# mLSTM keys and values brought to the rows of their chunk by a block-wise load and a VectorE transpose, in place of TensorE transposes

## What is computed

```python
s = jnp.einsum('bjhd,bshd->bhjs', q, k) * w
num = jnp.einsum('bhjs,bshe->bjhe', s, v) + inter_blh[..., None] * jnp.einsum('bjhd,bhde->bjhe', q, C)
den = jnp.sum(s, axis=-1).transpose(0, 2, 1) + inter_blh * jnp.einsum('bjhd,bhd->bjh', q, n)
h = num / jnp.maximum(jnp.abs(den), floor)[..., None]
C_new = decay[..., None, None] * C + jnp.einsum('bhs,bshd,bshe->bhde', w_last, k, v)
n_new = decay[..., None] * n + jnp.einsum('bhs,bshd->bhd', w_last, k)
```

## Time and profile before

| | us |
|---|---|
| median of three executions | 1893.55 |
| the profiled execution's own time | 1891.67 |
| its span (first to last instruction) | 1889.9 |
| TensorE busy | 1871.4 (99%) |
| VectorE busy | 1331.9 (70%) |
| ScalarE busy | 873.5 (46%) |
| the mLSTM's steps, first to last transpose | 572.3 to 817.8 |

### The profile page before, as it was taken

One profiled execution on the slowest core, in us unless ns is written; L12 is line 12 of the kernel. 1 busy time (PEld: TensorE's weight loads), 2 busy tenths in 40 slices (PEclk: granted clock), 3 DMA queues, 4 the chain that ended last, 5 costly groups with the idle time before them and its releaser, 6 DMA issues.

```text
span 1889.9 us, 33104 instructions
## 1 busy us (share of the span) xinstructions
PE 1871.4 (99%) x13219; PEld 1847.9 (98%) x13219; DVE 1331.9 (70%) x1975; ACT 873.5 (46%) x1601; POOL 110.5 (6%) x165
## 2 busy tenths in 40 slices
PE   9999999999999999999999999999999999999997
PEld 8999999999999999999999999999999999999997
DVE  7788999999997654783455479877776776636363
ACT  5554434544554456661222455644544454535342
POOL 0011111111111111110000000000000000000000
PEclk9999999999999999999999999999999999999999
DMA  4556676667656655559431341222121213556654
GB/s 136 160 141 150 161 190 167 158 176 184 191 165 203 203 156 159 156 167 242 123 140 45 120 138 67 81 70 91 69 81 69 92 69 128 177 204 203 213 171 158
DMA packets 155864, 272.86 MB, mean 144 GB/s; under 512 B 55997, under 2 KB 91837, under 8 KB 155713
## 3 DMA queue, kind: packets, MB, share of 16 engines
q1 hardware_dynamic: 140592, 235.16, 37.1%
q0 software_dynamic: 15120, 35.59, 10.6%
HBM read 206.97 MB, written 63.74 MB: 143 GB/s over the span
## 4 chain that ended last, share of the span: by engine, by line
PE 89%; DVE 5%; DMA 3%; issue 1%; ACT 1%; SPq 0%; POOL 0%; DVEq 0%; ACTq 0%; POOLq 0%
PE ps L1198 9%; PE ps L1200 9%; PE ps L1199 9%; PE ps L1352 7%; PE ps L1353 7%; PE ps L1354 7%; PE ps L1549 7%; PE ps L1547 7%; PE ps L1548 7%; PE ps L1569 4%; PE ps L1571 4%; PE ps L1570 4%; PE ps L1289 1%; PE ps L1286 1%; DMA araw<-wts 1%
## 5 line engine op out<-in xcount | busy, mean ns | idle before, releaser
L1198 PE MATMUL ps<-rx,fhi 128*128 128x368 f32 (+2 forms) x736 | 248.2, 337 | 0.8 <-ACT spl L1722 0.6
L1200 PE MATMUL ps<-rx,flo 128*128 128x368 f32 (+2 forms) x736 | 237.5, 323 | 0.0
L1199 PE MATMUL ps<-rx,fhi 128*128 128x368 f32 (+2 forms) x736 | 237.3, 322 | 0.0
L1352 PE MATMUL ps<-rx,ahi 128*128 128x304 f32 (+1 forms) x672 | 194.3, 289 | 0.4 <-DVE v L2570 0.3
L1353 PE MATMUL ps<-rx,ahi 128*128 128x304 f32 (+1 forms) x672 | 193.7, 288 | 0.0
L1354 PE MATMUL ps<-rx,alo 128*128 128x304 f32 (+1 forms) x672 | 193.6, 288 | 0.0
L1569 PE MATMUL ps<-ghi,dhi 128*128 128x384 f32 (+1 forms) x528 | 173.2, 328 | 2.7 <-DVE glo L2934 1.9
L1570 PE MATMUL ps<-glo,dhi 128*128 128x384 f32 (+1 forms) x528 | 172.3, 326 | 0.0
L1571 PE MATMUL ps<-ghi,dlo 128*128 128x384 f32 (+1 forms) x528 | 172.2, 326 | 0.0
L2927 DVE TENSOR_TENSOR dlo<-draw,dhi 128x1408 fp32r<-128x1408 f32 x48 | 77.8, 1624 | 118.3 <-ACT dhi L2136 118.3
L1198 PEld LDWEIGHTS ps<-rx,fhi 128*128 128x128 f32 x736 | 138.4, 188 | 2.8 <-ACT spl L1722 0.9
(11 more groups left out here) (364 smaller groups left out, 5701.8 us busy)
## 6 DMA issues: line engine op xcount, KB each, us to landing
draw<-wdn SPq DMA_DIRECT2D x48, 704.0 KB, 4.2
araw<-wts SPq DMA_DIRECT2D x105, 256.0 KB, 4.4
uraw<-wts SPq DMA_DIRECT2D x44, 512.0 KB, 4.3
fraw<-wts SPq DMA_DIRECT2D x27, 512.0 KB, 3.8
qkv<-scr_qkv SPq DMA_DIRECT2D x22, 544.0 KB, 8.9
scr_g<-cva SPq DMA_DIRECT2D x22, 512.0 KB, 2.6
alo<-wts POOLq DMA_DIRECT2D x42, 256.0 KB, 5.6
graw<-scr_g SPq DMA_DIRECT2D x43, 192.0 KB, 4.1
```

Of the source, the lines that this page charges most:

```text
L1198: pe.matmul(b, hi[:, w], src[:, his[k], cols], start=(k == 0), stop=False)
L1199: pe.matmul(b, hi[:, w], src[:, los[k], cols], start=False, stop=False)
L1200: mm = pe.matmul(b, lo[:, w], src[:, his[k], cols], start=False, stop=(k == KB - 1))
L1352: pe.matmul(b, ahi[s][:, c], bhi[:, k, :], start=(fresh and k == 0), stop=False, skip_group_check=True)
```

## The change

Keys and values are no longer loaded into `qkv` and transposed by TensorE. For each step SyncE's queue brings 128 columns of the four blocks of k and v from DRAM in squares of 32x32, with four DMAs, so that each square already lies in the place of its transpose (`kvq`, two buffers); one VectorE transpose by 32x32 blocks (`turn`) then gives k and v with tokens on the partitions (`kvt`). ScalarE multiplies the weight onto the keys in place one slot later (`weighted_keys`).

```diff
-C_HI = (12, 14, 0, 2, 4, 6, 8, 10)
+C_HI = (12, 14, 0, 8, 4, 6, 2, 10)
...
-                for b in range(4):
+                for b in range(2):
                     sp.dma_start(qkv[0][:, b, :], scr_qkv[0, b]).then_inc(qk_in, 16)
...
-                    sp.wait_ge(qk_in, 64 + 96 * (h - 1))
+                    sp.wait_ge(qk_in, 32 + 64 * (h - 1))
                     sp.wait_ge(nq_full, NSTEP * (h - 1))
-                for b in range(6):
+                for b in (0, 1, 4, 5):
...
+            def load_squares(i):
+                h, j = STEPS[i]
+                at = step_cols(j).start
+                if i >= 2:
+                    sp.wait_ge(turned_set, i - 1)
+                for b in range(4):
+                    sp.dma_start(kvq[i % 2][32 * b:32 * b + 32, :, :],
+                                 scr_qkv[h, 0:4, :, at + 32 * b:at + 32 * b + 32].rearrange("k (a q) n -> q (k a) n", q=32))\
+                        .then_inc(kvq_in[i % 2], 16)
...
             for s, ((kind, k), c) in enumerate(SLOTS):
+                i = step_at(s, -1)
+                if i is not None:
+                    load_squares(i)
...
+                        elif C_HI[j] == 8:
+                            sp.wait_ge(gate_act, 6)
+                            sp.wait_ge(gate_dve, 16)
+                        elif C_HI[j] == 2:
+                            sp.wait_ge(turned_set, len(STEPS))
...
             def scores(i):
-                if i == 0:
-                    pe.wait_ge(gt_set, 5)
...
                 if i:
-                    pe.wait_ge(kv_copied, 2 * i)
                     pe.wait_ge(a_set, i)
-                for b in range(4):
-                    mm = pe.transpose(bank(2, b * P, P), q[:, b, cols], ident[:, :])
-                mm.then_inc(kv_full, 1)
...
                 pe.wait_ge(a_set, i + 1)
-                pe.wait_ge(kv_copied, 2 * i + 2)
+                pe.wait_ge(kw_set, i + 1)
...
             def scores(i):
-                act.wait_ge(kv_full, i + 1)
-                if i >= 2:
-                    act.wait_ge(n_full, i - 1)
-                act.activation(vt[p][:, 0:DH], bank(2, DH, DH), ACT.Copy).then_inc(kv_copied, 1)
-                act.activation(kw[p][:, :], bank(2, 0, DH), ACT.Copy, scale=gt[:, 16 * j + 12 + h:16 * j + 13 + h])\
-                    .then_inc(kv_copied, 1)
                 act.wait_ge(w_neg, i + 1)
                 act.activation(wt[p][:, :], wt[p][:, :], ACT.Exp).then_inc(w_exp, 1)
+
+            def weighted_keys(i):
+                if i == 0:
+                    act.wait_ge(gt_set, 5)
+                act.wait_ge(turned_set, i + 1)
+                act.activation(kvt[p][:, 0:DH], kvt[p][:, 0:DH], ACT.Copy, scale=gt[:, 16 * j + 12 + h:16 * j + 13 + h])\
+                    .then_inc(kw_set, 1)
...
-                act.activation(zt[p][:, :], hn[p][:, 0:DH], ACT.Square, accum_out=sm[p][:, 3:4]).then_inc(ssq, 1)
+                act.activation(bank(2, 0, DH), hn[p][:, 0:DH], ACT.Square, accum_out=sm[p][:, 3:4]).then_inc(ssq, 1)
...
+                i = step_at(s, 1)
+                if i is not None:
+                    weighted_keys(i)
                 i = step_at(s, 0)
                 if i is not None:
                     scores(i)
...
+            def turn(i):
+                p = i % 2
+                if i >= 2:
+                    dve.wait_ge(n_full, i - 1)
+                dve.wait_ge(kvq_in[p], 32 + 64 * (i // 2 + 1))
+                dve.transpose(kvt[p][:, 0:2 * DH], kvq[p][:, :, :].rearrange("p a n -> p (a n)")).then_inc(turned_set, 1)
...
                     exponents(i)
                     scores(i)
+                    turn(i)
```

More of the change, by code:

```diff
@@ L453, in build @@
     qkv = [Room(at_rz + s * 6 * blk)(f"qkv{s}", [P, 6, T]) for s in range(2)]
+    room = Room(at_rz + 2 * blk)
+    kvq = [room(f"kvq{s}", [P, 16, 32]) for s in range(2)]
+    assert room.at <= at_rz + 4 * blk
     room = Room(at_rz + 6 * blk)
@@ L469, in build @@
     cb = [room(f"cb{s}", [P, 2, VW]) for s in range(2)]
-    vt = [room(f"vt{s}", [P, VW]) for s in range(2)]
-    kw = [room(f"kw{s}", [P, DH]) for s in range(2)]
+    kvt = [room(f"kvt{s}", [P, DH + VW]) for s in range(2)]
     wt = [room(f"wt{s}", [P, L]) for s in range(2)]
@@ L615, in build @@
         v1_out = sem("v1_out")
-        kv_full = sem("kv_full")
+        turned_set = sem("turned_set")
         s_full = sem("s_full")
-        kv_copied = sem("kv_copied")
+        kw_set = sem("kw_set")
         w_neg = sem("w_neg")
@@ L697, in build @@
         y_sto = [sem(f"y_sto{s}") for s in range(2)]
+        kvq_in = [x_in[4], x_in[5]]
         block = ctx.enter_context(nc.Block())
@@ L794, in load_head, with store_head @@
                 else:
-                    sp.wait_ge(qk_in, 64 + 96 * (h - 1))
+                    sp.wait_ge(qk_in, 32 + 64 * (h - 1))
                     sp.wait_ge(nq_full, NSTEP * (h - 1))
-                for b in range(6):
+                for b in (0, 1, 4, 5):
                     sp.dma_start(qkv[h % 2][:, b, :], scr_qkv[h, b]).then_inc(qk_in, 16)
+            def load_squares(i):
[7 more added lines that the diff above has]
+                        .then_inc(kvq_in[i % 2], 16)
+            def store_head(i):
+                h, j = STEPS[i]
+                first = 0 if j < NCHUNK else L - DEC
+                sp.wait_ge(zs_set, i + 1)
+                sp.dma_start(scr_z[h, step_cols(j)][first:L], zs[i % 2][first:L, :]).then_inc(z_out[i % 2], 16)
             def pairs():
@@ L842, in pairs @@
                 weights(N_A + 2)
[L844 to L848, removed]
             def load_nb(i):
@@ L922, in _ @@
                 if i is not None:
+                    store_head(i)
+                i = step_at(s, 4)
+                if i is not None:
                     h, j = STEPS[i]
-                    store_head(i)
                     if j == NCHUNK:
@@ L1149, in _ @@
             for s in range(2):
-                pool.memset(vt[s][:, DH:VW], 1.0).then_inc(const_set, 1)
+                pool.memset(kvt[s][:, 2 * DH:DH + VW], 1.0).then_inc(const_set, 1)
             pool.wait_ge(const_set, 15)
@@ L1276, in values @@
                 c = cb[j // NCHUNK]
+                vt = kvt[p][:, DH:DH + VW]
                 pe.wait_ge(a_set, i + 1)
-                pe.wait_ge(kv_copied, 2 * i + 2)
+                pe.wait_ge(kw_set, i + 1)
                 if i:
@@ L1286, in values @@
                         pe.matmul(bank(5, 0, VW), qkv[h % 2][:, 4 + b, cols], c[:, b, :], start=(b == 0), stop=(b == 1))
-                pe.matmul(bank(4, 0, VW), wt[p][:, :], vt[p][:, :], start=True, stop=True).then_inc(nq_full, 1)
+                pe.matmul(bank(4, 0, VW), wt[p][:, :], vt, start=True, stop=True).then_inc(nq_full, 1)
                 for b in range(2):
-                    mm = pe.matmul(bank(6 + b, 0, VW), kw[p][:, b * P:(b + 1) * P], vt[p][:, :], start=True, stop=True)
+                    mm = pe.matmul(bank(6 + b, 0, VW), kvt[p][:, b * P:(b + 1) * P], vt, start=True, stop=True)
                 mm.then_inc(n_full, 1)
@@ L1669, in values @@
                 act.wait_ge(hn_set, i + 1)
-                if i >= 2:
-                    act.wait_ge(zs_set, i - 1)
-                act.activation(zt[p][:, :], hn[p][:, 0:DH], ACT.Square, accum_out=sm[p][:, 3:4]).then_inc(ssq, 1)
+                if i:
+                    act.wait_ge(ssq, i)
+                act.activation(bank(2, 0, DH), hn[p][:, 0:DH], ACT.Square, accum_out=sm[p][:, 3:4]).then_inc(ssq, 1)
             def normed(i):
```

8 lines of the change are left out of this document (5 added, 3 removed).

## The result

The changed kernel took 1909.06 us (median of 4 runs, 1907.48 to 1909.37) against 1892.63 us for the kernel before, measured beside it (4 runs, 1889.69 to 1895.24). The ratio is 1.0086, with an interval of 1.0068 to 1.0103: it is slower by 16 us. The forecast was 1881.5, within 1876.5 to 1889.0.

What follows compares the result with a forecast made beforehand. TensorE was taken as the bound (busy 99%, 89% of the chain), VectorE nearly level late in the stage. 15.7 + 1.0 - 3.0 - 0.4 - 0.2 - 1.0 = 12.1 us off 1893.55 gave 1881.5, range 1876.5 to 1889.0.

Steps and rivals of the forecast that it cites:

- 15.7 us off TensorE: mLSTM steps: removing 144 transposes, four in each of 36 steps, saves 0.435 us per step on TensorE.
- The late stage, -3.0 -0.4: Last seven steps: VectorE sets the pace, so 3.0 us of the saving bring nothing and 0.4 us is lost.
- 1.1 to 1.3 later: Late stage: TensorE's `values` of 792.38, with 0.23 us in hand, comes this many us later, relative to the shifted kernel.
- The turn, 0.65: VectorE, each step: the new 512-column transpose costs 0.65 us, between 0.36 and 0.72; about 0.45 returns from shorter exponent waits.
- DMA engines at 0.85 to 0.90: mLSTM stage: expected DMA engine share, from 6.0 us of DMA work in a slot of 6.65.
- Rival (c): Steps: dearer 128-byte packets make DMA engines the bound; about 1907 us at 26 ns, about 1920 at 29.4; chance 0.08.
- Over 11 us for a landing of 7.1: Squares, issued two steps ahead, have over 11 us to land in 7.1, so hidden except behind a head's load.
- 1.7 for four issues: SyncE's queue: 1.7 us to issue a step's four square DMAs, subtracted from the 13.2 us until they are needed.
- `scr_z` stores 3 to 4 us later, margins of 1.5 to 3 us, 1.0 in all: SyncE's queue: stores stand behind squares; VectorE already waits in four places; margins to TensorE leave 1.0 us lost.
- Every rival: Four alternatives to the forecast: 1877.3 us (chance 0.20), 1887.5 (0.16), about 1907 to 1920 (0.08), 1893 (0.06, with small remainders).
- I am wrong if ... TensorE idles in the middle of the stage: Mid mLSTM stage: TensorE idle time there was named as one of three signs that the forecast is wrong.
- the 20 that I had named: VectorE's turn: total DMA waits over 20 us were named as a sign that the forecast is wrong.

Runs made afterwards that it cites:

- e15: e14 with each step's squares read as 2 KB packets from other places, leaving out the right keys and values; 1880.02 us, ratio 0.9927 to the kernel before.
- e14: Changed kernel with squares of steps 0 and 1 loaded with the first head, and four buffers each for turned rows and `nb`; 1883.99 us, ratio 0.9950.
- e7: Changed kernel with first squares early, four buffers for turned rows, and 2 KB packets from other places (right keys and values left out); 1884.79 us.
- e3: Changed kernel with the same four DMAs and bytes per step in 2 KB rows from other places, leaving out the right keys and values; 1893.73 us.
- e4: Changed kernel with VectorE turning only 32 of a step's 512 columns, the others left out; 1907.50 us, ratio 1.0086 to the kernel before.

## Why the prediction was wrong, step by step

- **15.7 us off TensorE: right.** It is 0.44 us in each undisturbed slot, and 1.85 instead of 1.42 at the first step (a start that scatters: in the other kernels with the change it is 0.0 to 3.0 us ahead). e15, nearest to a kernel in which only this happens, is 13.4 us ahead at the last step.
- **The late stage, -3.0 -0.4: the right kind of loss, priced too high.** In e14 TensorE's lead on the kernel before is 769.02 - 760.24 = 8.8 us at step 28 and 817.88 - 807.88 = 10.0 at step 35; in e15 it is 12.2 and 13.4. The last seven steps brought 1.2 us, not -0.4; they gave back 1.8, not 3.4. VectorE did not set the pace of all seven. Two `values` show it (e14, TensorE):

```profile
769.01 1.11 PE L1317 MATMUL ps<-cb,qkv 128*128 128x257 f32 x4 [0.41 <-ACT kvt L1691]
...
783.69 1.11 PE L1317 MATMUL ps<-cb,qkv 128*128 128x257 f32 x4 [1.16 <-ACT kvt L1691]
```

  The first stood at 778.12 before and waited 0.46 us; I had added 0.65 and 0.3 to that, and it waits 0.41. The second, before at 792.38, was to come 1.1 to 1.3 later and waits 1.16, though for the weighted keys and not for the update.
- **The turn, 0.65: measured 0.70** (36 of 699 to 711 ns), the next start after 0.63. VectorE took it in, as said: its wait for the exponent fell from 30.0 to 15.0 us.
- **DMA engines at 0.85 to 0.90: right**, 0.79 in the kernel with its stalls and 0.86 in e14. From the DMA view of 580 to 850 us, 72,073 more packets on the hardware queue took 19.2 more points of 16 engines (q1 of the kernel before, then after: packets, MB, share):

```profile
q1 hardware_dynamic: 18020, 33.67, 35.7%
```

```profile
q1 hardware_dynamic: 90093, 37.76, 54.9%
```

  That difference is net of the v blocks, which are no longer loaded, so it is no price of a packet. By the records of the packets themselves 71,332 of 128 bytes took 13.6 ns in the mean, 22.4 points of the share, close to the 14.7 that I took. The Trainium skill, "DMA: Bandwidth & Descriptors", Specifications, had spoken for a price out of proportion. For the bytes it is one: 128 in 13.6 ns are 9.4 GB/s an engine, and a packet of 4352 bytes, at 187 ns, makes 23. But the engines did not become the bound. Rival (c) named the right range of time by a mechanism that did not occur, which is luck; its own sum at 26 ns, moreover, gives 1904 (34 slots of 0.33 us, less the first wait), not 1907.
- **"Over 11 us for a landing of 7.1": wrong at the start of the stage.** Landings of squares were 3.3 us in the median but up to 12.6, and I had compared a median. The margin was also counted with "1.7 for four issues"; they took 1.9 at best and up to 7.42.
- **"The `scr_z` stores 3 to 4 us later, margins of 1.5 to 3 us, 1.0 in all": the step that failed, by its price.** The shift itself was right: the stores landed 3 us later in the mean. But in four places VectorE already waited for a store, and there 3 to 4 us more go over a margin of 1.5 to 3, a stall by the prediction's own numbers. Eight stores were waited for, 15.7 us in all. With the squares' wait at the start and the clock behind the stalls, the DMA term is some 30 us, not 1.
- **The start of the stage was not looked at.** I checked squares behind a head's load, not those of steps 0 and 1, which have no earlier slot's turn behind which to be issued, and which meet the opening loads: 10.8 us of wait.
- **The clock was left out.** Every rival was priced as idle time with the clock unchanged. Where TensorE had stalled the granted clock was 0.61 to 0.80 over 8 us, which cost up to 12 us in sum; in e14, whose longest wait is 1.3 us, it is 1.00. The Trainium skill, "TensorE: Matmul & The Clock Gate", Part 1, says that the clock has two levels and that an engine which was idle for long enough goes on at the lower one; the matmuls of 0.51 us behind the stall agree with that. So a stall can cost more than its length. Not each does: in e7 TensorE stood still for 2.43 us before 594.55 and the clock stayed at 1.00.
- "I am wrong if ... TensorE idles in the middle of the stage" was the sign that came true; the turn's wait for DMA, 10.8 us, stayed under the 20 that I had named.

Open: why SyncE's issue takes so long at times, and whether another engine's queue would spare it (not tried); how the 15 us of the small packets divide between the queue and the engines; and where the 4 us lie that e14 still lacks against e15.

## What to carry to other kernels

When work is moved from a compute engine to many small loads, price the queue that issues them, not only the engines that carry them: list every other transfer on that queue for which somebody waits, and give each a buffer more *before* judging the change. With two buffers each the change cost 16 us; with four for the stores and for the offsets, and the first squares asked for early, it brought 9 to 10. When a removed wait reappears under another name (`scr_z`, then `nb`), the cause is upstream of both, and both need the buffers at once.

## What the runs showed of the hardware

- **Issuing DMAs of 512 packets holds SyncE.** One takes between 303 ns and 5.3 us to issue, 489 ns in the median (144 of them, after), and the `nb` load of 64 KB behind them 2.5 us at 663.96 where it took 0.49 at 592.06. With 32 long rows per DMA (e3) a group of squares never took more than 3.4 us between 580 and 850 us, against 7.42 here at 580.99. In all SyncE issued for 187 of 246 us in the changed kernel, for 118 with the long rows and for 53 before. Why the issue is held, the trace doesn't show.
- **A VectorE transpose of 512 float32 columns takes 0.70 us** against 0.44 for 256: 1.0 ns a column over a fixed 0.18. The 32 columns of e4, at 0.20, lie on the same line.
- **The median landing of a store can fall while the stores come later:** from issue to landing `scr_z` took 3.3 us (7.1 before), but from turned rows to landing 11.7 us in the mean (8.7 before), because it left SyncE late. The time to landing has to be counted from when the data are ready.
